# Softmax attention: the four low-part splits of the merge weights done by VectorE between its row maxima instead of by GpSimd

## The reference, cut to what matters

```python
# 8 heads of 64 in 2 key/value groups of 4; q and k with partial rope; t <= 512
p_s = masked_softmax(q_pos @ k_slc.T, causal);  o_s = p_s @ v_slc
p_w = masked_softmax(q_pos @ k_win.T, causal);  o_w = p_w @ v_win
o_a = g0 * o_c + g1 * o_s + g2 * o_w            # o_c: attention over compressed blocks
gate_a, gate_b = split(sigmoid(h @ w_merge))    # 2 x 1024 columns
merged = gate_a * (o_a @ w_up_nsa) + gate_b * (o_b @ w_up_gla)
x = x + merged @ w_out
```

## Time and profile before

| what | value |
| --- | --- |
| median of 3 runs | 1589.5 us (1589.07 to 1591.51) |
| the profiled execution | 1590.72 us, of it 1588.9 us span of instructions |
| TensorE matmuls busy | 1500.3 us, 94% |
| VectorE busy | 800.2 us, 50% |
| ScalarE busy | 515.6 us, 32% |
| GpSimd busy | 154.7 us, 10% |
| mean granted TensorE clock | 0.974 of full speed |
| the loop of the change | about 946 to 1106 us of the span |

### The profile page before, as it was taken

One profiled execution on the slowest core, in us unless ns is written; L12 is line 12 of the kernel. 1 busy time (PEld: TensorE's weight loads), 2 busy tenths in 40 slices (PEclk: granted clock), 3 DMA queues, 4 the chain that ended last, 5 costly groups with the idle time before them and its releaser, 6 DMA issues.

```text
span 1588.9 us, 18834 instructions
## 1 busy us (share of the span) xinstructions
PE 1500.3 (94%) x6986; PEld 1206.4 (76%) x6986; DVE 800.2 (50%) x1003; ACT 515.6 (32%) x669; POOL 154.7 (10%) x114
## 2 busy tenths in 40 slices
PE   4999989699999999879989899999998999999997
PEld 3888768388888888648777587777886888888885
DVE  5899663654234343453583745455436334434434
ACT  4222343434332232234442323233224332212223
POOL 0030013000000000200140202120220000000001
PEclk9999999799999999989999999999999999999999
DMA  5333213032332332412331011010232233233221
GB/s 149 107 106 102 83 54 106 27 101 85 106 98 89 105 106 80 144 62 80 80 79 57 27 54 54 1 53 0 79 106 77 82 106 90 95 106 97 88 79 53
DMA packets 138116, 129.18 MB, mean 81 GB/s; under 512 B 14581, under 2 KB 134636, under 8 KB 138060
## 3 DMA queue, kind: packets, MB, share of 16 engines
q1 hardware_dynamic: 135552, 124.27, 25.1%
q0 software_dynamic: 992, 3.47, 0.7%
q10 hardware_dynamic: 1516, 0.69, 0.2%
HBM read 126.32 MB, written 2.10 MB: 81 GB/s over the span
## 4 chain that ended last, share of the span: by engine, by line
PE 88%; DVE 7%; ACT 2%; issue 2%; DMA 1%; POOL 0%; ACTq 0%; DVEq 0%; POOLq 0%
PE gemm L373 68%; PE gemm L707 3%; PE gemm L477 2%; PE misc L734 2%; PE misc L719 2%; PE gemm L400 2%; DVE rstd L1238 1%; PE misc L727 1%; PE misc L720 1%; PE misc L431 1%; DMA conv_rows<-in_conv_w 1%; DVE q_level L1535 1%; PE gemm L405 1%; PE misc L562 1%; DVE w_lo L1229 1%
## 5 line engine op out<-in xcount | busy, mean ns | idle before, releaser
L373 PE MATMUL gemm<-h_hi,w_hi 128*128 128x512 f32 x1152 | 454.1, 394 | 1.9 <-DVE w_lo L1229 1.9
L373 PE MATMUL gemm<-h_lo,w_hi 128*128 128x512 f32 x1152 | 450.4, 391 | 0.0
L373 PE MATMUL gemm<-h_hi,w_lo 128*128 128x512 f32 x1152 | 450.2, 391 | 0.0
L1229 DVE TENSOR_TENSOR w_lo<-w_raw,w_hi 128x2048 fp32r<-128x2048 f32 x112 | 257.5, 2299 | 191.7 <-ACT w_hi L821 191.6
L821 ACT ACTIVATE w_hi<-w_raw 128x2048 fp32r<-128x2048 f32 x116 | 221.4, 1909 | 144.0 <-PE gemm L373 136.1
L373 PEld LDWEIGHTS gemm<-h_hi,w_hi 128*128 128x128 f32 x1152 | 217.7, 189 | 51.6 <-issue 3.3
L373 PEld LDWEIGHTS gemm<-h_hi,w_lo 128*128 128x128 f32 x1152 | 217.6, 189 | 45.9
L373 PEld LDWEIGHTS gemm<-h_lo,w_hi 128*128 128x128 f32 x1152 | 217.7, 189 | 45.4 <-issue 0.8
L373 PE MATMUL gemm<-f_hi,w_hi 128*128 128x512 f32 x432 | 168.0, 389 | 0.0
L373 PE MATMUL gemm<-f_lo,w_hi 128*128 128x512 f32 x432 | 168.0, 389 | 0.0
L373 PE MATMUL gemm<-f_hi,w_lo 128*128 128x512 f32 x432 | 168.0, 389 | 0.0
(11 more groups left out here) (295 smaller groups left out, 1646.8 us busy)
## 6 DMA issues: line engine op xcount, KB each, us to landing
w_raw<-in_w_in SPq DMA_DIRECT2D x62, 512.0 KB, 4.5
w_raw<-in_w_up SPq DMA_DIRECT2D x32, 512.0 KB, 4.4
w_raw<-in_w_down SPq DMA_DIRECT2D x32, 512.0 KB, 4.3
w_raw<-in_w_ffn_gate SPq DMA_DIRECT2D x22, 512.0 KB, 4.5
w_raw<-in_w_ffn_up SPq DMA_DIRECT2D x22, 512.0 KB, 4.5
w_raw<-in_w_ffn_down SPq DMA_DIRECT2D x16, 512.0 KB, 4.1
w_raw<-in_w_o SPq DMA_DIRECT2D x8, 512.0 KB, 4.1
w_raw<-in_w_out SPq DMA_DIRECT2D x8, 512.0 KB, 3.9
```

The source lines that it names most:

```text
L373: mm = nc.tensor.matmul(bank[:], w[par][:, kt, col0:col0 + P], x(n), start=first, stop=last)
L1229: V.tensor_tensor(WLO[par][:, 0:kts, :], RAW[par][:, 0:kts, :], f(WHI[par][:, 0:kts, :]), SUB).then_inc(S("lo_done"), 1)
```

## The change

VectorE's loop gets a `split_lo` after step 1 (behind copy(1, 1) and row_max(2, 1), ahead of copy(2, 0)) and after step 9 (ahead of copy(10, 0)) of each pass; GpSimd's loop loses its four splits with their two waits each. Slabs, buffers and semaphore counts stay; `split_lo` waits for `hi_done` alone.

```diff
@@ VectorE @@
+        sM = PH["merge_a"][0]
         with dve.Fori(0, 2) as i:
             step.enter(i, 2 * 16 + 2 * TT)
...
                     V.tensor_copy(PT[g][:, 0:w], M[2][:, 0:w]).then_inc(read[2], 1)
                     if s < 4 * TT - 1:
                         row_max(s + 1, g)
+                if s % 8 == 1:
+                    split_lo(sM + t // 2 + 1, (sM + t // 2 + 1) % 2, i)
                 if s % 4 < 3:
                     continue
@@ GpSimd @@
-        sM = PH["merge_a"][0]
         with pool.Fori(0, 2) as i:
             for t in range(TT):
-                if t % 2 == 0:
-                    s = sM + t // 2 + 1
-                    pool.wait_ge(S("hi_done"), s + 1 + 2 * i)
-                    pool.wait_ge(S("lo_done"), s + 2 * i)
-                    Q.tensor_tensor(WLO[s % 2][:], RAW[s % 2][:], f(WHI[s % 2][:]), SUB).then_inc(S("lo_done"), 1)
                 pool.wait_ge(read[3], 17 + t + 1 + 4 * i)
                 Q.tensor_tensor(OA[:, t, :], OA[:, t, :], OTMP[:], ADD).then_inc(S("oa_added"), 1)
```

## The result

The changed kernel takes 1593.27 us (median of 12 runs, 1592.04 to 1595.18) against 1589.70 (median of 12 runs, 1588.89 to 1591.51): a ratio of 1.0022 with a 95% interval of 1.0013 to 1.0031, so it is slower by 3.5 us, within 2.1 to 4.9. Forecast were 1592.0 us in a range of 1590.0 to 1594.6; the time lies in it, and slower by over 0.2% had 0.35 of the chance, less than no visible change. The profiled execution took 1592.43 us, of it 1590.6 of span.

The account below looks back on a forecast made before the run. TensorE's matmuls were taken to bound the loop. Two passes losing 0.90 and 0.34 us each add 2.5 us to the 1589.5 us median, giving 1592.0 us, range 1590.0 to 1594.6; removing GpSimd's splits brings nothing.

Parts of the forecast that it names:

- Nobody waits for GpSimd's split: In the loop, removing four GpSimd splits of 4545 ns brings nothing, since no engine of the core waits for them.
- A split of 2.29 us fits no pause: VectorE idles only 0.70 and 1.09 us ahead of the copies of steps 2 and 10, so the split delays them.
- delay behind step 1: The transpose's weight load begins 1.08 us late; 0.18 comes back, so TensorE loses 0.90 us in each pass.
- loss behind step 9: The transpose's weight load begins 0.52 us late, of which TensorE loses 0.34 us in each pass.
- No second wait in the same step: After the late copy, copy(2, 1) is not later than the first made it, so nothing further is lost.
- High parts and loads have time: ScalarE's high parts are ready before VectorE asks; slab loads start 3.0 and 4.8 us later, at no cost.
- rival (d): Behind the loop, later work makes low clock stretches vanish: four give 6.8 us, leaving 1585.2 us; chance 0.04.
- Rival (b): Waits behind step 1's splits drop TensorE's clock to 1.2 GHz, 1.7 us per fall, 1595.4 us in all; chance 0.07.
- Rival (c): Shared SBUF interfaces: beside GpSimd work each VectorE split takes 3.20 us instead of 2.29, giving 1595.6 us; chance 0.03.

Follow-up runs that it names:

- kt = 1: Changed kernel with an eighth of each of the four VectorE splits made once more ahead of it: 1628.4 us, ratio 1.0242.

## Why the prediction was right, and where it was not

- **Nobody waits for GpSimd's split; its removal brings nothing.** Right: taken away alone, the loop is 159.37 against 159.34.
- **A split of 2.29 us fits no pause and delays the copy, then the transpose of group 1.** Right, at the four places named, with one wait each. The terms: delay behind step 1 forecast 1.08, measured 1.11; loss 0.90, measured 0.94 and 0.96; loss behind step 9 0.34, measured 0.35 twice; sum 2.5, measured 2.6. The small rest is the start of the split, 0.04 us before the instruction ahead of it ends where the working took 0.08.
- **No second wait in the same step.** Right: copy(2, 1) follows the shift, and the next way from mask to mask is 1.42, where it was 1.41. The exponential of step 3 comes 0.26 us later against its mask matmul than before (957.12 and 957.09, before 957.35 and 957.58), but no transpose waits for it.
- **High parts and loads have time.** Right: no wait for `hi_done`, and the loads show nowhere.
- **On the median.** 2.5 was forecast and about 3.1 to 3.6 came; 0.5 of the difference stands in the part behind the loop. The working priced that part at nothing in the forecast and put it into rival (d), as a gain of 5.7 us and more with a chance of 0.04. The mechanism is real, but in the size of a single fall that goes or grows, and in either direction: +0.5 us for a shift of 2.6, -1.2 to -1.6 for shifts of 0.8 to 1.5. It belonged into the sum's own range. With it, by my estimate, the chance of slower by over 0.2% would have been nearer a half.
- **Rival (b), the clock in the loop.** The clock held, so the rival did not come in, but the argument against it did not carry. It was that a wait with 0.67 us of matmuls in 2 us had left the clock up and that the new wait leaves more work around it; with kt = 1 TensorE was busy for 3.82 of 5 us, and the clock fell. Its price was wrong too: 1.7 us for each fall, read from a fall in dense products at the end of the loop. Inside the loop a fall lasts tens of microseconds, and the runs with longer holds show 35 to 90 us. A range that took this in would have been no better for this change, but an engineer would have to know the price: a first wait 0.46 us longer than the changed kernel's (1.61 against 1.15) already brought it.
- **Rival (c), contention.** It did not come in, as GpSimd was idle at the splits. Where it was forced, it fell on GpSimd's addition, which began second, and not on VectorE's split as in the row that priced it, where the split began second.
- **The Trainium skill's choice of engine** (GPSIMD Engine Reference, section Engine selection: elementwise work on tiles on VectorE, about twice as fast). The speed agrees, 2292 against 4545 ns; what decided was that four times 4545 ns on an engine for which nobody waits cost nothing, and four times 2292 ns on one that stands between two steps of TensorE cost 2.6 us. The other sentence of this page of the Trainium skill (Key points: GpSimd shares its SBUF interfaces with VectorE, with contention for VectorE instructions with two SBUF inputs) agrees with the 3.24 us of the addition here.

## What to carry to other kernels

Before moving work to a faster engine, take that engine's slack at the very place (the time from its last instruction to the moment at which the busiest engine would stop, less the instruction in between) and cut the work into pieces that fit: 2.3 us in one piece cost up to 0.96 each, in two pieces nothing. Where the busiest engine's work is short matmuls with gaps, do not price a new wait of this size at its own length alone, but test how far its clock is from falling: here waits of 1.15 left it up, and 0.46 us more at each of the four places cost 35 in the median. And a difference of a microsecond or two in the median of a kernel whose clock changes on its way is to be checked against the stage's own length in the trace, which repeated within 0.1 us.

## What was not expected of the hardware

- The granted clock, once down to 1.2 GHz at a wait of 1.6 to 3.5 us behind steps 1 to 3, stayed down for 38 to 116 us while TensorE showed busy 5.00 of 5 us. Behind step 13 (w = 512) it came back within 10 us, in another kernel's step 12 (also w = 512) only after 34. A wait of 2.42 us elsewhere in the same loop left it up. What decides was not settled.
- A shift of the loop's end by 0.8 to 1.5 us removed a fall of the clock behind the loop, and one of 2.6 us did not: the part behind it took 480.7 to 481.1 us in the first case and 482.7 to 482.8 in the second, against 482.3 without a shift.
- Contention between VectorE and GpSimd fell on whichever instruction began second: a VectorE split took 3.20 us when a window sum had begun 0.01 us before it, but 2.28 us when it began 0.16 to 0.17 us ahead of an addition, and that went from 1.26 to 3.24.
